# A bitwise top-k search inside a hybrid attention layer, split into two searches that take turns

## The reference

```python
# A: gated DeltaNet, 4 heads x 128: conv + SiLU on q, k, v, then a chunked scan over the state
_, o = lax.scan(step, s0, xs)
# B: sparse attention; a light indexer scores all keys, the best 256 of each query are kept
score = jnp.einsum('bqjs,bqj->bqs', jax.nn.relu(logits), wi * IDX_HEADS ** -0.5)
score = jnp.where(causal[None], score, -jnp.inf)
_, idx = lax.top_k(score, topk)                 # topk = 256
# C: cross-attention, 4 heads x 64, into 256 memory tokens
y = jnp.concatenate([o_a, o_s, o_m], axis=-1) @ w_out[l]
x = _layernorm(DEEPNORM_ALPHA * x + y, ln_g[l], ln_b[l])
```

## Time and profile before

| | |
|---|---|
| median of 3 runs | 853.98 us (852.0 to 854.2) |
| the profiled execution | 854.07 us, its span in the trace 852.3 us |
| PE busy in the span | 90% |
| ACT, DVE, POOL busy | 54%, 58%, 18% |
| mean granted PE clock | 0.96 of full |
| first and last count | 167.6 us, 492.4 us |

### The profile page before, as it was taken

One profiled execution on the slowest core, in us unless ns is written; L12 is line 12 of the kernel. 1 busy time (PEld: TensorE's weight loads), 2 busy tenths in 40 slices (PEclk: granted clock), 3 DMA queues, 4 the chain that ended last, 5 costly groups with the idle time before them and its releaser, 6 DMA issues.

```text
span 852.3 us, 11425 instructions
## 1 busy us (share of the span) xinstructions
PE 765.4 (90%) x3996; PEld 622.0 (73%) x3996; DVE 495.9 (58%) x1068; ACT 461.4 (54%) x1045; POOL 152.3 (18%) x248
## 2 busy tenths in 40 slices
PE   6999969899997999989997999876698998998975
PEld 5888858777886788778886788663566776774764
DVE  5633868755655565564655487843556456636532
ACT  4433566789777975998778932233443333332310
POOL 0000000063112510233112610001003033302330
PEclk9999979999998999999998999997899999999998
DMA  9312110123201330023001231009102112120201
GB/s 358 103 50 75 49 38 26 37 66 103 65 26 56 75 104 25 27 77 106 26 26 56 74 116 50 36 28 349 58 1 74 44 56 87 67 63 33 75 25 49
DMA packets 56424, 60.87 MB, mean 71 GB/s; under 512 B 16048, under 2 KB 42928, under 8 KB 55984
## 3 DMA queue, kind: packets, MB, share of 16 engines
q1 hardware_dynamic: 56368, 60.15, 21.4%
HBM read 45.46 MB, written 14.68 MB: 71 GB/s over the span
## 4 chain that ended last, share of the span: by engine, by line
PE 58%; DVE 17%; ACT 14%; issue 8%; DMA 2%; SPq 1%; POOL 0%; DVEq 0%; ACTq 0%; POOLq 0%
PE bank L870 16%; PE bank L878 8%; PE bank L880 8%; PE bank L879 8%; ACT cst L1697 5%; PE bank L884 3%; PE bank L1114 2%; PE bank L1142 2%; PE bank L1034 2%; PE bank L1049 2%; PE bank L1021 2%; PE bank L1047 2%; ACT ring_split L1614 2%; DVE score L1317 1%; DVE mix_lo L1564 1%
## 5 line engine op out<-in xcount | busy, mean ns | idle before, releaser
L878 PE MATMUL bank<-x_hi,ring_split 128*128 128x512 f32 x480 | 199.6, 416 | 7.8 <-DVE x_lo L1262 7.3
L880 PE MATMUL bank<-x_hi,ring_split 128*128 128x512 f32 x480 | 191.1, 398 | 0.0
L879 PE MATMUL bank<-x_lo,ring_split 128*128 128x512 f32 x480 | 190.5, 397 | 0.0
L1697 ACT ACTIVATE cst<-score,sel 128x1024 bf16<-128x1024 f32 (+2 forms) x192 | 166.8, 873 | 24.0 <-DVE sel L1339 24.0
L878 PEld LDWEIGHTS bank<-x_hi,ring_split 128*128 128x128 f32 x480 | 92.4, 192 | 24.2 <-DVE ring_split L1270 7.9
L880 PEld LDWEIGHTS bank<-x_hi,ring_split 128*128 128x128 f32 x480 | 92.0, 192 | 20.3
L879 PEld LDWEIGHTS bank<-x_lo,ring_split 128*128 128x128 f32 x480 | 92.3, 192 | 15.2
L1798 ACT ACTIVATE arena<-arena,misc 128x512 f32<-128x512 f32 (+7 forms) x32 | 24.8, 775 | 80.9 <-DVE misc L1534 80.9
L1614 ACT ACTIVATE arena<-bank 128x512 f32<-128x512 f32 (+1 forms) x108 | 49.7, 499 | 34.5 <-PE bank L884 10.5
L870 PE MATMUL bank<-w_out_hi,mix_hi 128*128 128x512 f32 x128 | 56.4, 441 | 6.7 <-DVE mix_lo L1564 4.2
L1872 POOL TENSOR_TENSOR arena<-arena,hsc 128x512 f32<-128x512 f32 x8 | 9.2, 1149 | 275.9 <-ACT arena L1754 275.9
(11 more groups left out here) (246 smaller groups left out, 1453.4 us busy)
## 6 DMA issues: line engine op xcount, KB each, us to landing
ring<-in_w_groups SPq DMA_DIRECT2D x30, 512.0 KB, 3.5
x_raw<-in_x_t SPq DMA_DIRECT2D x8, 512.0 KB, 9.3
side_z<-stage SPq DMA_DIRECT2D x16, 256.0 KB, 2.0
w_out_sb<-in_wout_t SPq DMA_DIRECT2D x2, 2048.0 KB, 12.4
zgT<-side_z SPq DMA_DIRECT2D x8, 512.0 KB, 3.9
qkvT<-in_x SPq DMA_DIRECT2D x8, 512.0 KB, 4.8
out_y<-arena SPq DMA_DIRECT2D x8, 512.0 KB, 2.8
ring<-in_wmem_t SPq DMA_DIRECT2D x2, 1024.0 KB, 4.8
```

The costliest lines, as they stand in the source:

```text
L878: nc.tensor.matmul(dst, hi, xh, start=(c == 0), stop=False)
L879: nc.tensor.matmul(dst, hi, xl, start=False, stop=False)
L880: last = nc.tensor.matmul(dst, lo, xh, start=False, stop=(c == KT - 1))
L1697: sc.activation(signs[order[e] % 2][:, 0:w], score[:, score_at(b):score_at(b + 1)], ACT.Sign, scale=-1.0, bias=candidate[:, b - 2:b - 1], ...
```

## The change

- The search becomes two: set 0 is blocks 2 to 5 (columns 0 to 3 of the small tiles), set 1 is blocks 6 and 7 (columns 4 and 5). In each iteration come the pairs (5, 2), (4, 3), (7, 6).
- Each set has its own update and its own semaphore `candidates_ready`. An update is placed once two fill points have passed since its set's last count, and a set's next counts are placed only after its update.
- The operation that multiplied by the sign in each update is gone, and so is the one that made `candidate`: `n_wanted` is multiplied by the sign once, and the counts read `bits_tried` as bias and the sign (negated, in `score_scale`) as a scale that is a column of a tile, where the scale was the number -1.
- `SELECT_RATE` is 0.79. The last 6 of the 192 counts are placed after `At` of the last head, and write to `hbuf`. The distances are loaded when the first 186 are done, at the step `At`, ahead of `diag_load` in SP's queue.
- `reach`, `threshold` and `dm` are placed one pair per fill point, those of set 1 last.

```diff
-COUNT_GROUPS = ((7, 2), (6, 3), (5, 4))
+COUNT_GROUPS = (((5, 2), (4, 3)), ((7, 6),))
+SET_COLUMNS = (slice(0, 4), slice(4, 6))
...
-SELECT_RATE = 0.82
+SELECT_RATE = 0.79
...
+    def update(n, at_once=False):
+        if due[n] and (at_once or point[0] > due[n][1] + 1):
+            add(due[n][0])
+            due[n] = None
+
+    def count():
+        n, group = searches.pop(0)
+        plan.extend(group)
+        if group[-1][2] == COUNT_GROUPS[n][-1][-1]:
+            due[n] = (("update", group[-1][1], n), point[0])
+
+    def counts():
+        if owed[0] >= 1 and searches and not due[searches[0][0]]:
+            owed[0] -= 1
+            count()
+
+    def mark():
+        n = len(marks) <= len(last_marks)
+        if marks and not any(m == n for m, _ in searches) and not due[n]:
+            for e in marks.pop(0):
                 add(e)
...
             owed[0] += SELECT_RATE
-            update()
+            point[0] += 1
+            for n in range(2):
+                update(n)
...
             if silus[0] == 0:
-                owed[0] -= select(int(owed[0] >= 1))
+                counts()
             silus[0] = 0
+            if ("At", DNH - 1, 1) in plan:
+                mark()
...
-                if e == ("reach", 7):
-
-                    sp.wait_ge(keys_counted, N_SEL * FLOAT_BITS)
+                if e == ("At", DNH - 1, 1):
+
+                    sp.wait_ge(keys_counted, counts_in_heads)
                     sp.dma_start(cst[:, C_KT:C_BIT], consts[:, C_KT:C_BIT]).then_inc(kt_sem, 16)
...
-                        link(v.tensor_tensor(n_off, n_off, t_sign, ALU.mult))
-                        link(v.tensor_scalar(bit_kept.bitcast(U32), n_off, 0.0, float(1 << bit), ALU.is_lt, ALU.mult))
+                        link(v.tensor_scalar(kept.bitcast(U32), off, 0.0, float(1 << bit), ALU.is_lt, ALU.mult))
                         if bit:
-                            link(v.scalar_tensor_tensor(bits_tried.bitcast(U32), bit_kept.bitcast(U32), cst[:, C_BIT + bit - 1:C_BIT + bit].bitcast(U32),
-                                                        bits.bitcast(U32), ALU.bitwise_or, ALU.bitwise_or))
-                            v.tensor_tensor(candidate, bits_tried, t_sign, ALU.mult).then_inc(candidates_ready, 1)
-                        link(v.tensor_tensor(bits.bitcast(U32), bits.bitcast(U32), bit_kept.bitcast(U32), ALU.bitwise_or))
+                            v.scalar_tensor_tensor(tried.bitcast(U32), kept.bitcast(U32), cst[:, C_BIT + bit - 1:C_BIT + bit].bitcast(U32),
+                                                        bits_.bitcast(U32), ALU.bitwise_or, ALU.bitwise_or).then_inc(candidates_ready[n], 1)
+                        link(v.tensor_tensor(bits_.bitcast(U32), bits_.bitcast(U32), kept.bitcast(U32), ALU.bitwise_or))
...
-                    sc.activation(signs[order[e] % 2][:, 0:w], score[:, score_at(b):score_at(b + 1)], ACT.Sign, scale=-1.0,
-                                  bias=candidate[:, b - 2:b - 1], accum_out=n_low[:, b - 2:b - 1]).then_inc(keys_counted, 1)
+                    tried, scale = (bits_tried, score_scale[:, b - 2:b - 1]) if it else (candidate, -1.0)
+                    if order[e] > counts_in_heads:
+
+                        act.wait_ge(conv_done, 6 * DNH)
+                    to = (signs_last if order[e] > counts_in_heads else signs)[order[e] % 2]
+                    sc.activation(to[:, 0:w], score[:, score_at(b):score_at(b + 1)], ACT.Sign, scale=scale,
+                                  bias=tried[:, b - 2:b - 1], accum_out=n_low[:, b - 2:b - 1]).then_inc(keys_counted, 1)
```

More of the change, by code:

```diff
@@ L209, in make_plan @@
             add(u)
-    owed, silus = [0.0], [0]
+    silus = [0]
     def woven(steps, todo):
@@ L298, in make_plan @@
     first = BLOCK_ORDER[0]
-    update()
-    while selection:
-        select()
-        update()
+    while searches or any(due):
+        for n in range(2):
+            update(n, True)
+        if searches:
+            count()
+    while marks:
+        mark()
     for e in [("cT", 0), ("cT", 1), ("deltanet_scale", first), ("qabs", first), *[t for h in range(SAH) for t in scores(first, h)], ("msc", first, 0), ("msc", first, 1)]:
```

87 lines of the change are left out of this document (43 added, 44 removed).

## The result

The changed kernel takes 854.64 us (median of 20 runs, 849.48 to 858.37), the kernel before 852.15 (20 runs, 849.50 to 855.14). The ratio is 1.0028, 95% interval 1.0016 to 1.0040: slower by 0.28%, which is within the 0.3% that counts as no change. The forecast of 844.5 us is 10 us too low. It started from 854.07 us, the profiled execution, and promised 9.55 us less; against the median of the 20 runs before, 2.5 us are lost, so the change itself was misjudged by 12 us.

A forecast was written before the change was run, and what follows sets the result against it. PE, busy 90% of the span, was taken as the bound, losing time where it waits or runs slowly. 854.07 - 21.65 (turns) + 7.2 (new waits) + 1.5 (dearer counts) + 3.4 (last head) = 844.5 us; range 836 to 855.

The forecast's parts named there:

- Part 1: At the three turns between heads, PE's waits for the copy `vnew` all go: 13.4 us won.
- The half clock that goes with them: Around the turns' 3.8 us waits PE runs at 1.2 GHz; this ends with the waits, winning 8.25 us.
- Part 2: At each turn PE newly waits 2.1 us for ACT's `KBT` copies and 0.3 for `vnew`: 7.2 us in all.
- Part 3: The scale column makes each of 186 ACT counts 90 ns dearer, 16.7 us of ACT; 1.5 us charged.
- Part 4: DVE does 64 updates of four operations for 32 of six: 14 us more DVE work, nothing charged.
- Part 5: In the last head, `reach` and `threshold` cost the scan 3.4 us; the second long last update is charged nothing.
- Part 6: In SP's queue the distances go ahead of `diag_load` and wait for 186 counts; nothing charged.
- The sum: Whole kernel: 854.07 - 21.65 + 7.2 + 1.5 + 3.4 = 844.5 us.
- (a): Rival: the new 2.1 us waits at the turns keep the clock low; 850 to 853 us, chance 0.22.
- (c): Rival: ACT becomes the bound at the turns and scans, and the kernel is slower; 863.5 us, chance 0.13.
- (b): Rival: ACT has room, the scale is nearly free and the `KBT` copies are in time; 835.8 us, chance 0.15.

The follow-up runs named there:

- run 66: Not a run's label: in the changed kernel's two series (854.64 and 853.92 us) the median run has 66 and 70 us at 1.2 GHz.
- the two versions with cheap counts: Split order, `XY` first in the last head, constant scale: with six-operation updates 844.81 us; with the changed kernel's four-operation updates, sign left out, 839.58 us.
- the dear counts in the old order: The kernel before with only the counts' scale read from a tile column holding -1.0: 864.53 us, ratio 1.0143.
- The run with a free scale: The changed kernel with constant -1.0 as the counts' scale, sign left out, so negative thresholds are not searched rightly: 844.24 us, ratio 0.9904.
- the changed kernel once more: The changed kernel, unedited, run again for a second profile: 853.92 us, ratio 1.0013 to the kernel before.

## Why the prediction was wrong

**Part 1, the waits of 3.8 us go: right.** 13.4 us became 3.0, with none left at step 1. **The half clock that goes with them: right at its place, wrong in the sum.** At the turns the changed kernel's clock is 1.00, and the traces of both orders say that it is the order that does this. But 8.25 us were taken off the whole. First, that is more than its own rows give: PE worked 14.0 of those 16.5 us, and a wait for another engine is not made longer by PE's clock, so 7.0. Second, part of it came back in the last head. Third, it was read from one execution. The profiled execution before had 70 us at 1.2 GHz, the median run of the same kernel 64 (c = 0.9625, 26 runs). The changed kernel's profiled execution has 54, its median run 66 to 70. In which places the median run has the other 12 to 16 us no trace here shows.

**Part 2, 2.4 us of new wait per turn: about right in size, partly wrong in kind.** The turns show 2.46, 3.57 (1.10 + 0.94 + 1.53) and 2.81 us (0.92 + 1.89), 8.8 in all for 7.2. At the first turn the `KBT` copies start at 266.94, where the forecast had 267.05; but PE comes there at 267.04 and not at 265.5, because it has waited for DVE twice already. So less than half of the 8.8, 0.62 + 1.53 + 1.89, is the wait for the copies; the rest comes from DVE, some of it from updates beside POOL's work. The wait of 2.2 us for the copies at the start of head 0, 0.6 before, is no effect of the change: it is 2.19 or 2.20 in all six traces in which the clock stays at 1.00 there, one of the old order among them, and shorter in the seven in which it falls, since a slower PE comes later.

**Part 3, a count dearer by 90 ns: right. What that is worth: wrong.** The mean of a count, 965 ns against 873, is 92 ns more. The Trainium skill (ScalarE: Activation LUTs, the part on the instruction's timing) says about 93 per pointer operand, and the trace agrees. I had this row right and charged 1.5 us for it, with 2.7 more inside part 2 (three turns of ten counts). Runs give 10 us in the new order, 12.7 in the old. The step that failed is the sentence that the 16.7 us come "in a stretch where 24.0 us of waiting is to go". ACT's waits for updates fell only from 24.0 to 10.1 us, while its work in that stretch rose by 18.6 (264.6 to 283.2), and the copies that PE needs stand behind the counts in ACT's order. That each of a head's counts makes them later is read from that order. No single wait holds the 10 us, which is why the rows of one turn did not show them.

**Part 4, DVE 14 us more at no cost: the size was wrong (26), the cost is not settled.** More than half of the 26 is not in the number of operations but in their length. In 168 to 494 us, 24 of the changed kernel's operations on the small tiles took over 0.35 us, 24.3 us together; in the kernel before 8 did, 7.5 us. The 16 more would have been 2.7 us at the usual 0.17; so 14 of the 26 us are their being held up. What that costs the kernel no run separates.

**Part 5, the last head: the step that failed.** The scan itself was priced at 3.4 us and grew by 4.1 (2.3 more wait, the rest about what 3.4 us at half clock cost). But the second long last update was dismissed with "35.7 of 42 us busy leaves 6.3 for them". That compares sums over a window, and DVE works in order. From 497.08 to 503.72 us it did nothing but search operations, with `XY` behind them and PE behind `XY`: 4.2 us. Putting `XY` first is worth 8 us in the changed kernel, and 4.6 and 4.7 in the two versions with cheap counts, where the wait was 3.1 and 2.7.

**Part 6, SP's queue: right.** No wait of PE for a DMA appears in the last head.

**The sum.** In the two profiled executions PE is idle 852.3 - 765.4 = 86.9 us before and 847.7 - 760.3 = 87.4 after, +0.5; and its busy time falls by 5.1. The waits, term by term: -13.4 + 8.8 (three turns) + 1.6 (start of head 0) + 1.2 (`XY` behind the copy of `M`) + 2.3 (scan) + 4.2 - 1.2 (ahead of `M`, new less old) = +3.5 us; less 2.0 of waits in head 0 that only the first trace has (0.66 ahead of `M` at 213.06, 1.35 behind `oall` at 295.75), and less about 1 outside of the heads. At full clock the forecast had -13.4 + 7.2 + 1.5 + 3.4 = -1.3. So about 2 us of the error are waits, the one ahead of `M` above all; 3.2 are the 8.25 us of clock, of which at most 5.1 came. The other 7.1 us lie between the profiled pair, 4.6 us faster, and the medians, 2.5 slower: the profiled execution before was 1.9 us above its kernel's median, that after 5.2 below. The clocks go the same way, 0.959 against a median of 0.9625 before, and 0.968 against 0.959 and 0.961 after. More than that is open.

**The rivals.** None had the mechanism. (a) gave the best time, 850 to 853 us, but by a low clock at the turns, which is not there. (c), ACT as the bound, had 863.5 us; its price is real (864.5 us with the dear counts in the old order), but the changed kernel stays clear of it. (b), "the scale is nearly free", is refuted by the rows. The run with a free scale came to 844.2, the forecast's own number, and the measured 854.64 lies just inside the forecast's outer range of 836 to 855; both are luck, since the parts do not add up that way.

## What to carry to other kernels

Do not set new operations against an engine's idle time in a window: write out what stands behind them in that engine's order, and who waits for that; here 6.3 idle us in a window of 42 did not prevent a wait of 4.2. A cost of 90 ns per instruction on an engine whose copies feed the next one is to be multiplied out first: of 17 us it cost 6 to 13 here, with no single wait to show it. And a clock term taken from one profiled execution wants the mean clocks of the other runs beside it before it is added up; where PE waits for another engine next, a low clock ahead of that wait may cost nothing.

## What the runs showed of the hardware

**Small DVE operations are held by POOL's long ones.** An update operation takes 0.15 to 0.23 us. All 24 that took over 0.35 us in 168 to 494 us lie beside a POOL operation: 20 end within 0.04 us of its end, the other four in the middle of a row that stands for two POOL operations. The clearest case, in the changed kernel:

```profile
199.04 2.54 POOL L1889 TENSOR_TENSOR arena<-arena,cst 128x512 f32<-128x512 f32 x2
199.21 2.39 DVE L1347 TENSOR_TENSOR sel<-sel 128x4 f32<-128x4 f32 x1 [4.68 <-ACT cst L1727]
201.63 0.17 DVE L1360 TENSOR_SCALAR sel<-sel 128x4 uint32<-128x4 f32 x1
```

The subtraction of four columns ends at 201.60, POOL's pair at 201.58; the next operation takes 0.17 us. The Trainium skill (SBUF — State Buffer, "Who interferes with whom") says that DVE and GpSimd share a port pair that one of them holds for a whole instruction; the trace agrees. It also says that an operation with one SBUF input is held only if it runs in a mode of two ports; L1360 has one input and took 0.97 us at 254.21, in the rows of the first turn; in which mode it ran no trace shows. That the port is the cause was not tested here by moving POOL's work. In the search of 61 small updates 24 operations were held up, in that of 31 updates 8.

**A second pointer operand costs about as much as the first**, 92 ns per `ACTIVATE` (1141 against 1233 ns at 1024 columns), and nearly the same at 384 columns: 90 ns (606 against 696). The first cost 95 in the earlier trace rows.

**The clock falls in some executions and not in others, at the same place.** All thirteen traces have a wait of 2.7 us at about 170 us, in steps that are the same in all but for the search's. Behind it the granted clock is 0.50 for 3.4 to 6.8 us in seven of them, and stays at 1.00 in six. The low stretch costs next to nothing there: `U` starts at 176.29 us in a trace at full clock, behind a wait of 2.19 us for ACT, and at 176.38 in one with 3.4 us at half clock, behind a wait of 0.60 (the changed kernel once more, and the one with `XY` first).

**The mean clock tells only a part of how runs of one kernel differ.** In the 20 runs of the changed kernel it is 0.957 to 0.968, and the slower runs mostly have the lower clock. But span times mean clock is not constant: it is 820.6 and 819.8 us in the fastest and the slowest run (849.5 and 858.4 us), and 815.9 to 823.4 over all of them.
